# Gate and up projections of a decoder layer as seven half-size products per column tile

## The reference

```python
x = x + rms_norm(mix, post_mix_g[i])

f = rms_norm(x, pre_ffn_g[i])
f = (jax.nn.silu(f @ w_ffn_gate[i]) * (f @ w_ffn_up[i])) @ w_ffn_down[i]
x = x + rms_norm(f, post_ffn_g[i])

e = p[i] @ w_ple_up[i]
gate = jax.nn.sigmoid(x @ w_ple_gate[i])
x = x + rms_norm(gate * e, ple_norm_g[i])
```

## Time and profile before

| | |
|---|---|
| device time, median of three runs | 1637.91 us (1636.59 to 1638.6) |
| span of the profiled execution | 1633.5 us |
| PE busy, PEld busy | 1547.8 us (95%), 1234.5 us (76%) |
| DVE, ACT, POOL busy | 837.1 us (51%), 521.7 us (32%), 245.0 us (15%) |
| gate and up, tiles 2 to 21 | 824.8 to 1259.9 us of the span |
| down, 44 steps | 1259.9 to 1503.4 us |

### The profile page before, as it was taken

The page is one execution under the profiler, slowest core; times in us unless marked ns, Lnnn a source line. Parts: engine busy times, 40 slices in busy tenths (PEclk is TensorE's granted clock), DMA queues, the critical chain, the costliest instruction groups (busy, mean ns, idle before and its releaser), DMA issues.

```text
span 1633.5 us, 19991 instructions
## 1 busy us (share of the span) xinstructions
PE 1547.8 (95%) x7448; PEld 1234.5 (76%) x7448; DVE 837.1 (51%) x1218; ACT 521.7 (32%) x1001; POOL 245.0 (15%) x368
## 2 busy tenths in 40 slices
PE   6999999987789899999999999999999999999997
PEld 5887788876655666656788888888888888887886
DVE  5658888986678999943321111111111335445553
ACT  5444433134543434344311110111111324433321
POOL 5444366238300000000000000000000000000000
PEclk9999999998999999999999999999999999999999
DMA  6222233252110000010321111111101111232110
GB/s 194 71 59 75 70 102 110 97 222 94 48 44 26 27 26 14 14 52 14 90 78 38 39 51 51 51 51 51 51 26 51 48 50 50 92 103 97 52 65 39
DMA packets 96481, 105.47 MB, mean 65 GB/s; under 512 B 7840, under 2 KB 72096, under 8 KB 96416
## 3 DMA queue, kind: packets, MB, share of 16 engines
q1 hardware_dynamic: 96416, 104.61, 20.7%
HBM read 85.72 MB, written 18.87 MB: 64 GB/s over the span
## 4 chain that ended last, share of the span: by engine, by line
PE 73%; DVE 10%; DVEq 6%; issue 5%; ACT 3%; POOL 3%; SPq 1%; DMA 0%; POOLq 0%; ACTq 0%
PE ps L528 20%; PE ps L530 20%; PE ps L529 20%; PE ps L754 4%; DVEq L1455 4%; DVE m L1452 3%; DVE lm L1544 2%; DVE sc L1441 2%; DVEq L1453 1%; PE ps L699 1%; PE ps L716 1%; PE ps L707 1%; ACT pt L1107 1%; PE ps L645 1%; PE ps L643 1%
## 5 line engine op out<-in xcount | busy, mean ns | idle before, releaser
L528 PE MATMUL ps<-fth,wh 128*128 128x512 f32 x704 | 274.5, 390 | 1.1 <-ACT ftr L1141 1.1
L529 PE MATMUL ps<-ftl,wh 128*128 128x512 f32 x704 | 274.0, 389 | 0.0
L530 PE MATMUL ps<-fth,wl 128*128 128x512 f32 x704 | 273.9, 389 | 0.0
L1603 DVE TENSOR_TENSOR ht<-sg,ps 128x512 f32 (+1 forms) x44 | 30.2, 687 | 366.8 <-ACT sg L1163 366.8
L1452 DVE MAX8 m<-sc 128x8 f32<-128x384 f32 (+5 forms) x192 | 171.1, 891 | 13.1 <-issue 2.9
L1454 DVE MATCH_REPLACE8 sc<-m,sc 128x384 f32<-128x384 f32 (+5 forms) x192 | 168.1, 876 | 0.3 <-issue 0.3
L528 PEld LDWEIGHTS ps<-fth,wh 128*128 128x128 f32 x704 | 132.1, 188 | 29.1 <-ACT ftr L1141 1.3
L1163 ACT ACTIVATE sg<-ps 128x512 f32<-128x512 f32 x44 | 26.3, 599 | 398.6 <-PE ps L530 398.6
L529 PEld LDWEIGHTS ps<-ftl,wh 128*128 128x128 f32 x704 | 132.1, 188 | 27.5 <-issue 0.2
L530 PEld LDWEIGHTS ps<-fth,wl 128*128 128x128 f32 x704 | 132.1, 188 | 27.5
L528 PE MATMUL ps<-dh,hth 128*128 128x512 f32 x352 | 137.3, 390 | 1.3 <-DVE htl L1658 1.3
(11 more groups left out here) (219 smaller groups left out, 2771.3 us busy)
## 6 DMA issues: line engine op xcount, KB each, us to landing
raw<-in_w_in SPq DMA_DIRECT2D x48, 256.0 KB, 3.1
dr<-in_w_ffn_down SPq DMA_DIRECT2D x44, 256.0 KB, 2.6
wr<-in_w_ffn_gate SPq DMA_DIRECT2D x21, 512.0 KB, 4.1
wr<-in_w_ffn_up SPq DMA_DIRECT2D x21, 512.0 KB, 5.3
ret_rows<-stg SPq DMA_DIRECT2D x32, 320.0 KB, 3.5
rp<-ret_rows SPq DMA_DIRECT2D x8, 1280.0 KB, 6.4
xn<-in_x SPq DMA_DIRECT2D x8, 512.0 KB, 5.2
wo<-in_w_out SPq DMA_DIRECT2D x1, 4096.0 KB, 20.1
```

What stands on the lines that cost most here:

```text
L528: pe.matmul(o, ah, wh, start=start, stop=False)
L529: pe.matmul(o, ah, wl, start=False, stop=False)
L530: return pe.matmul(o, al, wh, start=False, stop=stop)
```

## The change

Tiles 0 and 1 are computed as before. Of tiles 2 to 21, gate and up together are read as one product of two 2x2 block matrices: the weights' blocks are A11, A12 (gate, first and second 512 of the 1024 features), A21, A22 (up, the same), and the rows' blocks are the two halves of the features by the two halves of the 1024 rows. Such a product takes seven products of blocks (each 4 `mm3`) in place of eight, with 15 sums of blocks (Strassen's scheme in Winograd's form):

- Four sums of the rows' blocks, TS1 to TS4, are the same for all tiles. DVE makes them once (`sum_row`, 8 instructions), ACT and DVE split them (TH, TL).
- Four sums of the weights' blocks per tile, `weight_sums`, each 128x512, DVE. ACT and DVE split the gate weights, the four sums and A22 (3584 elements a partition in three instructions each, where it was 2048 in one).
- Seven products in the order 1, 6, 5, 7, 2, 4, 3 (`PRODUCTS`). Three open a bank; product 2 adds onto product 1, 7 and 4 onto 6, 3 onto 5, each after the sum before it has been read. Six banks are in use, three for a tile.
- Seven combining sums and products by DVE per tile (`row_half`: u2, u3, c22, c21, h1, c12, h2), and on ACT a copy (`first_term`) and two silus. c12, h2 and the second silu of a tile come while PE is on the next tile.
- The loops are gone: the programs of all engines are written out.

The hidden rows no longer stay in SBUF. Each tile's 128x1024 is stored to DRAM (512 KB), and each of the 44 down steps loads it again beside its weights (768 KB a step in place of 256 KB). The down operands have three buffers in place of two; the load of step n waits for the end of step n - 3 on PE. p is laid out transposed when it is passed in, so that the 16 PE transposes between the steps 21 and 22 fall away and it is loaded and split in SBUF during steps 6 to 10. Some buffers move, and the squares of the last stage use a buffer of their own.

The core of the diff:

```diff
+    RAWS = [sb(f"raws{i}", [P, 2, KT, P], a) for i, a in enumerate((60, 164))]
...
+    GH = [sb(f"gh{i}", [P, KT, P], a, F32R) for i, a in enumerate((68, 108))]
+    GL = [sb(f"gl{i}", [P, KT, P], a, F32R) for i, a in enumerate((60, 164))]
...
+    SS = [sb(f"ss{i}", [P, 4, 4, P], a) for i, a in enumerate((2, 188))]
+    SSL = [sb(f"ssl{i}", [P, 4, 4, P], a, F32R) for i, a in enumerate((2, 188))]
+    SSH = [sb(f"ssh{i}", [P, 4, 4, P], a, F32R) for i, a in enumerate((172, 196))]
...
+    HR = [sb(f"hr{i}", [P, S], a) for i, a in enumerate((60, 172, 2))]
...
+    PRODUCTS = (1, 6, 5, 7, 2, 4, 3)
...
+        def down(n):
+
+            dh, f = divmod(n, FT)
+            if n == 0:
+                sp.wait_ge(s["t_gu"], gu_at(FT - 2, 4))
+            elif n < 3:
+                sp.wait_ge(s["t_gu"], gu_at(FT - 2, 3))
+            else:
+                sp.wait_ge(s["t_dn"], n - 2)
+            if n < FT:
+                sp.wait_ge(st_h[f % 2], hidden_stored(f))
+            src = w_ffn_down[0, f * P:(f + 1) * P, dh * 512:(dh + 1) * 512]
+            sp.dma_start(DR[n % 3][:, :], src).then_inc(load_dr[n % 3], 16)
+            sp.dma_start(HR[n % 3][:, :], h_dram[f]).then_inc(load_dr[n % 3], 16)
+
+        for f in range(2):
+            store_hidden(f)
+        for g in range(G0, FT):
+            if g > G0:
+                store_hidden(g - 1)
+            if g + 2 < FT:
+                sp.wait_ge(s["t_gu"], gu_at(g, 4))
+                gate_up(g + 2)
+            if g == FT - 2:
+                down(0)
+        for n in range(1, 3):
+            down(n)
+        store_hidden(FT - 1)
+        sp.wait_ge(s["t_gu"], GU_ALL)
         for k in range(2):
             sp.dma_start(WGR[k][:, :], w_ple_up[0, k * P:(k + 1) * P, :]).then_inc(load_wg[k], 16)
...
+        def product_operands(g, m):
+
+            slot = g % 2
+            k0, k1 = slice(0, 4), slice(4, KT)
+            r1, r2 = slice(0, 512), slice(512, S)
+            if m == 1:
+                return GH[slot][:, k0, :], GL[slot][:, k0, :], FTH[0][:, k0, :], FTL[:, k0, r1]
+            if m == 2:
+                return GH[slot][:, k1, :], GL[slot][:, k1, :], FTH[0][:, k1, :], FTL[:, k1, r1]
+            if m == 3:
+                return SSH[slot][:, 3, :, :], SSL[slot][:, 3, :, :], FTH[1][:, k1, :], FTL[:, k1, r2]
+            if m == 4:
+                return UH[slot][:, :, :], UL[slot][:, :, :], TH[4][:, :, :], TL[4][:, :, :]
+            i = m - 5
+            return SSH[slot][:, i, :, :], SSL[slot][:, i, :, :], TH[i + 1][:, :, :], TL[i + 1][:, :, :]
+
+        def product_waits(g, m):
+
+            if m == 1:
+                pe.wait_ge(s["v_gl"], split_at(g, 0))
+                if g < G0 + 2:
+                    pe.wait_ge(s["v_ht"], 3)
+                else:
+                    pe.wait_ge(s["a_sg"], sg_at[("sg1", g - 2)])
+            elif m == 6:
+                pe.wait_ge(s["v_gl"], split_at(g, 1))
+                if g >= G0 + 2:
+                    pe.wait_ge(s["v_ht"], ev_at[("c21", g - 2)])
+                if g == G0:
+                    pe.wait_ge(s["v_tl"], 1)
+            elif m == 5:
+                if g >= G0 + 2:
+                    pe.wait_ge(s["v_ht"], ev_at[("c12", g - 2)])
+                if g == G0:
+                    pe.wait_ge(s["v_tl"], 2)
+            elif m == 7:
+                pe.wait_ge(s["v_ht"], ev_at[("u2", g)])
+                if g == G0:
+                    pe.wait_ge(s["v_tl"], 3)
+            elif m == 2:
+                pe.wait_ge(s["a_sg"], sg_at[("s1", g)])
+            elif m == 4:
+                pe.wait_ge(s["v_gl"], split_at(g, 2))
+                pe.wait_ge(s["v_ht"], ev_at[("u3", g)])
+                if g == G0:
+                    pe.wait_ge(s["v_tl"], 4)
+            else:
+                pe.wait_ge(s["v_ht"], ev_at[("c22", g)])
+
+        def product(g, m):
+            product_waits(g, m)
+            ah, al, bh, bl = product_operands(g, m)
+            o = bank({1: 0, 2: 0, 5: 2, 3: 2, 6: 4, 7: 4, 4: 4}[m] + g % 2)
+            opens = m in (1, 5, 6)
+            for k in range(4):
+                ins = mm3(o, ah[:, k, :], al[:, k, :], bh[:, k, :], bl[:, k, :], opens and k == 0, k == 3, not opens)
+            ins.then_inc(s["t_gu"], 1)
...
+        for g in range(G0, FT):
+            for m in PRODUCTS:
+                product(g, m)
...
+        def down(n):
             operands(n)
-            for r in range(RT):
-                m = row_product(slot, r, False, False)
-            m.then_inc(s["t_dn"], 1)
+            for r in FIRST_ROWS if n == 0 else range(RT):
+                if n == 0 and r == 0:
+                    pe.wait_ge(s["v_ht"], ev_at[("h2", FT - 2)])
+                if n == 0 and r == 1:
+                    pe.wait_ge(s["a_sg"], sg_at[("sg1", FT - 1)])
+                if n == 0 and r == 5:
+                    pe.wait_ge(s["v_ht"], ev_at[("c21", FT - 1)])
+                if n == 0 and r == 3:
+                    pe.wait_ge(s["v_ht"], ev_at[("c12", FT - 1)])
+                if n == FT:
+                    pe.wait_ge(s["a_fo" if r % 2 == 0 else "v_fo"], r // 2 + 1)
+                m = row_product(n, r, n % FT == 0, n % FT == FT - 1)
+                if n == FT - 1:
+                    m.then_inc(s["t_acc"], 1)
+            if n == FT - 1:
+                pe.wait_ge(s["t_acc"], RT)
+                pe.sem_inc(s["t_dn"], 1)
+            else:
+                m.then_inc(s["t_dn"], 1)
...
-        pe.wait_ge(s["load_pn"], 16)
-        for k in range(2):
-            pe.wait_ge(s["a_fo"], k + 1)
-            pe.wait_ge(s["v_fo"], k + 1)
-            for r in range(RT):
-                m = pe.transpose(pair(k)[:, r * P:(r + 1) * P], PN[:, r, k * P:(k + 1) * P], ID)
-            m.then_inc(s["t_pt"], 1)
...
+        def weight_sums(g):
+
+            raw, ss = RAWS[g % 2], SS[g % 2]
+            a11, a12, a21, a22 = raw[:, 0, K0, :], raw[:, 0, K1, :], raw[:, 1, K0, :], raw[:, 1, K1, :]
+            dve.wait_ge(load_wr[g % 2], weights_landed(g))
+            if g == G0:
+                dve.wait_ge(s["t_pv"], STEPS)
+            elif g == G0 + 1:
+                dve.wait_ge(s["t_gu"], 4)
+            else:
+                dve.wait_ge(s["t_gu"], gu_at(g - 2, 3))
+            v.tensor_tensor(ss[:, 0, :, :], a21, a22, ALU.add).then_inc(s["v_ws"], 1)
+            v.tensor_tensor(ss[:, 2, :, :], a11, a21, ALU.subtract).then_inc(s["v_ws"], 1)
+            dve.wait_ge(s["v_ws"], sums_at(g, 1))
+            v.tensor_tensor(ss[:, 1, :, :], ss[:, 0, :, :], a11, ALU.subtract).then_inc(s["v_ws"], 1)
+            dve.wait_ge(s["v_ws"], sums_at(g, 3))
+            v.tensor_tensor(ss[:, 3, :, :], a12, ss[:, 1, :, :], ALU.subtract).then_inc(s["v_ws"], 1)
+
...
+        def row_half(name, g):
+
+            a, b, c = bank(g % 2), bank(2 + g % 2), bank(4 + g % 2)
+            s1, u2, hb1, hb2 = S1B[g % 2][:, :], U2B[g % 2][:, :], HB[g % 2][:, 0:512], HB[g % 2][:, 512:S]
+            if name == "u2":
+                dve.wait_ge(s["t_gu"], gu_at(g, 6))
+                dve.wait_ge(s["a_sg"], sg_at[("s1", g)])
+                if g >= G0 + 2:
+                    after("h2", g - 2)
+                ins = v.tensor_tensor(u2, c, s1, ALU.add)
+            elif name == "u3":
+                dve.wait_ge(s["t_gu"], gu_at(g, 7))
+                if g == G0:
+                    dve.wait_ge(st_h[0], 16)
+                else:
+                    after("c22", g - 1)
+                ins = v.tensor_tensor(U3B[:, :], c, s1, ALU.add)
+            elif name == "c22":
+                after("u3", g)
+                if g >= G0 + 2:
+                    dve.wait_ge(st_h[g % 2], hidden_stored(g - 2))
+                ins = v.tensor_tensor(hb2, b, U3B[:, :], ALU.add)
+            elif name == "c21":
+                dve.wait_ge(s["t_gu"], gu_at(g, 4))
+                ins = v.tensor_tensor(hb1, c, s1, ALU.add)
+            elif name == "h1":
+                after("c21", g)
+                dve.wait_ge(s["a_sg"], sg_at[("sg1", g)])
+                ins = v.tensor_tensor(hb1, hb1, SG[0][:, :], ALU.mult)
+            elif name == "c12":
+                dve.wait_ge(s["t_gu"], gu_at(g, 3))
+                after("u2", g)
+                ins = v.tensor_tensor(u2, b, u2, ALU.add)
+            else:
+                dve.wait_ge(s["a_sg"], sg_at[("sg2", g)])
+                after("c22", g)
+                ins = v.tensor_tensor(hb2, hb2, u2, ALU.mult)
+            ins.then_inc(s["v_ht"], 1)
...
+        sum_row(1, 1)
+        sum_row(1, 2)
+        sum_row(3, 1)
+        for k in range(4):
             rows_lo(1, k)
+        sum_row(2, 0)
+        for k in range(4, KT):
+            rows_lo(1, k)
+        hidden(1, 0)
+        sum_row(4, 0)
+        sum_row(4, 1)
+        weight_sums(2)
+        sum_rows_lo(2)
+        weights_lo(2, 0)
+        sum_rows_lo(1)
+        hidden(0, 1)
+        sum_rows_lo(3)
+        weights_lo(2, 1)
+        sum_rows_lo(4)
+        weights_lo(2, 2)
+        hidden(1, 1)
+
```

(26 more changed lines are left out.)

561 lines of the change are left out of this document (303 added, 258 removed).

## The result

The changed kernel takes 1581.4 us (median of four runs, 1577.71 to 1583.49) beside 1638.26 us of the kernel before on the same chip (1636.59 to 1640.43): ratio 0.9647, with a 95% interval of 0.963 to 0.9664. The forecast was 1582.5 us. The profiled execution took 1583.49 us with a span of 1581.6 us; it is the longest of the four, whose other spans are 1578.2, 1580.9 and 1575.8 us.

What follows compares the result with a forecast made beforehand. PE was taken to bound the kernel: 54.4 us for removed matmuls plus 1.4 between down steps 21 and 22 less 0.5 for late loads, 55.3 off 1637.9, stated as 1582.5 us. Its own range was 1579 to 1586 us.

Steps and rivals of the forecast that it cites:

- The matmuls removed: Gate and up, tiles 2 to 21: 84 matmuls a tile instead of 96, 240 fewer at 226.6 ns, saving 54.4 us.
- DVE and ACT beside PE: In each tile, added work takes DVE 11.8 and ACT 5.4 of 19.04 us, costing nothing while the order holds.
- The margin at product 7: In each tile, u2 ends at 7.2 us and product 7 is due at 8.16: 0.9 us to spare, no stall.
- Late loads: Weight loads in the tile loop, now and then delayed by instruction fetches of about 1.3 us; 0.5 us cost in all.
- The switch: Entry into the FFN: row sums and splits added on DVE cost 0, with a margin of 2.4 us.
- The down steps: Each step's 768 KB load and operand preparation take 7.7 of 10.9 us: margin 3.2 us, cost 0.
- Step 21/22: Between these down steps, 3.45 us lost before and 2.1 after (bounds 0.46 and 3.2): 1.4 us gained.
- What lies around the span: Whole kernel: the median time is 4.4 us above the profiled span of 1633.5 us, and this stays.
- The range: Whole kernel's time: 1579 to 1586 us as the forecast's own range, with chance 0.80.
- A (product 7 waits): Tile loop: the chain from load to u2 exceeds its margin; 1 us of stall gives 1602 us; chance 0.12.
- B (hand-overs cost): Between products in the tiles: each hand-over drains the array, 0.46 us, 64 us in all, giving 1647 us; chance 0.03.
- C (down by its loads): Down steps: load chains over 10.9 us stretch three steps by the excess; 1 us too long gives 1596; chance 0.04.

Runs made afterwards that it cites:

- the first experiment: Product 5 of each tile issued twice, restoring the old matmul count, against the changed kernel; 1637.72 us, ratio 0.9991 to the kernel before.
- the late reload: Loads of down step n wait for the end of step n - 2 instead of n - 3, against the changed kernel; 1655.27 us, ratio 1.01.

## Why the prediction was right, by its steps

- **The matmuls removed, 54.4 us.** 54.4 measured, start to start, and 54.4 is what the eighth product gives back. The pitch of 226.6 ns held on both sides (380.80 us for 1680 matmuls is 226.7 ns). By the pitch that the Trainium skill states (TensorE: Matmul & The Clock Gate, the section on 56 ns against 53.3 ns), 215.8 ns for 512 columns, it would have been an estimated 51.8 us, 2.6 us short (and the time 1585.1 us by the forecast's other terms, where the prediction wrote 1584.5); the trace decides against it for these fp32r matmuls.
- **DVE and ACT beside PE, no cost.** Right. DVE is busy 58% of the tile (221.94 of 380.80), 62% forecast.
- **The margin at product 7, 0.9 us.** In the tile shown, the loads landed 3.13 us into the tile (forecast 3.3), u2 ended at 6.96 (7.2): 1.20 us to spare. Over the tiles it is 1.2 us in the mean, and 0.49 us at the least. Two experiments that shift the chain against product 7 by 2.7 us and two that lengthen it by 0.7 and 2.9 us agree with 1.1 to 1.2.
- **Late loads, 0.5 us.** Mis-sized: nothing, in twenty tiles of the changed kernel. But the tile with 0.49 us to spare shows that landings scatter by more than half a microsecond, and with one pass more in the chain two tiles of sixteen had a hole. The margin absorbed what the forecast paid for.
- **The switch, no cost.** Right. The half (1,0) starts 13.45 us behind (0,0), 13.47 before. The last operand of product 6 of tile 2 is the remainder of the weight sums, and it is done 3.8 us before the product starts:

```profile
827.07 2.28 DVE L1822 TENSOR_TENSOR ssl<-ss,ssh 128x2048 fp32r<-128x2048 f32 x1
...
833.12 0.39 PE L601 MATMUL ps<-th,ssh 128*128 128x512 f32 x1
```

  The forecast had this part done at 823.5 and wanted at 827.5, 4.0 to spare; both times are 5.6 to 5.9 us later in the profile after, because the FFN starts 5.6 us later.
- **The down steps, margin 3.2 us.** 3.0 in the step read above, mostly 2.5 to 4 over the others.
- **Step 21/22, 1.4 us gained.** 1.4 for the down steps as a whole (243.26 - 241.88), but by luck: the forecast took 3.45 us of loss before and 2.1 after, the profiles have 4.1 and 2.7, and the two errors cancel. Before, the two waits for a remainder cost 1.62 us from start to start where the earlier trace rows lists 1.3 as idle, and each hole has wider starts behind it, for which the forecast had no term. After, the mechanism is as forecast, casts ahead of copies; in this profile the load landed 5.1 us behind its first issue (1325.64 to 1330.71) where 4.6 was read off, and the hole is 2.5 us. It is not a fixed size: the seven profiles that keep this order of copies and three buffers have it at 1.6 to 2.5 us, with the 2.1 of the forecast among them. The lower bound, the drain of 0.46 us, was none: with the copies first nothing is lost.
- **The sum.** 55.3 us forecast against the shown 57.5 from the FFN to the end. The 2.2 us between them are the 0.5 for late loads that weren't needed and the 1.6 us of half clock in the last stage of the profile before, which no term of the forecast was about. By medians the gain is 56.9 us. That 1582.5 us lies within 1.1 us of the median is better than the terms deserve, given a spread of 6 us between four runs.
- **What lies around the span, 4.4 us.** This didn't touch the sum, since the saving was taken off the median, but it is not a constant that stays: in the runs with both numbers the time is about 1.9 us above the span (1583.49 - 1581.6). So the profiled execution of the kernel before was a shorter one than its median.
- **The range.** The forecast's own range of 1579 to 1586 us is said to come from the bounds. Added up, they give 1582.5 - 0.5 - 2.1 = 1579.9 and 1582.5 + 1.8 + 7.5 + 1.1 = 1592.9, so its upper end is 7 us too low for what it claims; the result didn't need it.
- **Rivals.** A (product 7 waits) did not come, but its law did, and it was too mild: past the margin each us of hole costs more than 20 us. The holes that three experiments made were 29.0, 32.0 and 30.9 us where the margin gave 29, 32 and 29. B (hand-overs cost) is excluded: 435.10 us for 140 products and 20 repeated ones in the first experiment. C (down by its loads) is one step of asking away, and then costs 74 us by medians (1655.27 - 1581.4).

What the forecast had no term for is the price of a stall beyond its length. In three kernels the holes of the loop were 29.0, 32.0 and 30.9 us and its twenty tiles took 33.2, 36.5 and 39.7 us more: 1.14, 1.14 and 1.28 times. With the late reload, the holes of the down steps were 54.2 us more than the changed kernel's and these steps took 68.2 more, 1.26 times. What makes the difference is how many pieces at half clock fell behind holes (1, 1, 4 and 6). Rival A's 1602 for 1 us of stall would have been an estimated 1605, from 0.14 us more a hole, before any half clock.

## What to carry to other kernels

Where one engine has no hole in the trace, count its instructions at their start-to-start pitch, and check the added work of the others not by its sum but along the one chain that ends at a bank or buffer about to be written again; the margin read from a timeline is the number that decides, and it should be read in all rounds of the loop, not in one (here 0.5 to 1.8 us). Put another product between the read of a bank and the product that adds onto it (without it this loop lost 1.6 us a tile), ask for reloads early enough for the whole way from issue to operands (7 to 8 us here, against a step of 5.44), and copy banks out before preparing operands that are wanted later. In this kernel a stall cost 1.14 to 1.28 times its length.
